# A decoder step on Trainium2: GpSimd makes every low part of the feed-forward weights, VectorE only the weight sums

## What is computed

```python
def conv_ffn(x, buf, w_up, conv_w, conv_b, w_down):
    u = x @ w_up                                   # 1024 -> 2 * 3072
    u_full = jnp.concatenate([buf.astype(u.dtype), u], axis=1)
    uc = causal_dwconv(u_full, conv_w, conv_b)     # width 3, per channel
    val, gate = uc[..., :D_FF], uc[..., D_FF:]
    return (jax.nn.gelu(gate) * val) @ w_down, new_buf
```

## Time and profile before

| what | before |
|---|---|
| median of 3 runs | 2521.88 us (2520.99 to 2522.19) |
| the profiled execution, its own time | 2521.42 us |
| its span, first to last instruction | 2519.5 us |
| TensorE busy | 2482.8 us, 99% of the span |
| VectorE busy | 1722.3 us, 68% |
| ScalarE busy | 1060.0 us, 42% |
| GpSimd busy | 852.7 us, 34% |
| chain that ended last | TensorE 79%, VectorE 5%, ScalarE 1% |
| mean granted TensorE clock | 0.998 of full speed |

### The profile page before, as it was taken

One profiled execution on the slowest core, in us unless ns is written; L12 is line 12 of the kernel. 1 busy time (PEld: TensorE's weight loads), 2 busy tenths in 40 slices (PEclk: granted clock), 3 DMA queues, 4 the chain that ended last, 5 costly groups with the idle time before them and its releaser, 6 DMA issues.

```text
span 2519.5 us, 41775 instructions
## 1 busy us (share of the span) xinstructions
PE 2482.8 (99%) x16340; PEld 2426.5 (96%) x16340; DVE 1722.3 (68%) x2796; ACT 1060.0 (42%) x1832; POOL 852.7 (34%) x527
## 2 busy tenths in 40 slices
PE   8999999999999999999999999999999999999998
PEld 7999999999999999998999999899999999999998
DVE  8877497666666666786655665649766666666678
ACT  5665253333333333334444444615333333333343
POOL 2001324344444333443333333032344443333341
PEclk9999999999999999999999999999999999999999
DMA  4111301111111111143233332411111111111112
GB/s 145 49 45 64 111 30 51 51 51 51 51 51 43 50 47 42 47 145 121 91 100 97 99 103 87 156 59 34 51 51 51 51 50 44 51 45 41 50 46 98
DMA packets 102769, 170.16 MB, mean 68 GB/s; under 512 B 11909, under 2 KB 50309, under 8 KB 102318
## 3 DMA queue, kind: packets, MB, share of 16 engines
q1 hardware_dynamic: 96622, 145.19, 18.1%
q10 hardware_dynamic: 5952, 22.30, 2.3%
HBM read 145.93 MB, written 26.23 MB: 68 GB/s over the span
## 4 chain that ended last, share of the span: by engine, by line
PE 79%; DVE 5%; ACT 1%; issue 1%; DVEq 0%; ACTq 0%
PE psum L1369 19%; PE psum L1225 13%; PE psum L1227 13%; PE psum L1226 13%; PE psum L1431 3%; PE psum L1435 3%; PE psum L1433 3%; PE psum L1465 2%; PE psum L1111 2%; PE psum L1489 2%; PE psum L1477 1%; PE psum L1668 1%; DVE line L2366 1%; DVE inverse_rms L2378 1%; DVE line L2326 0%
## 5 line engine op out<-in xcount | busy, mean ns | idle before, releaser
L742 POOL TENSOR_TENSOR w_lo<-w_raw,w_hi 128x512 fp32r<-128x512 f32 x232 | 372.9, 1608 | 771.6 <-ACT w_hi L1791 771.0
L1227 PE MATMUL psum<-xn_lo,w_hi 128*128 128x352 f32 x1568 | 506.7, 323 | 0.0
L1225 PE MATMUL psum<-xn_hi,w_hi 128*128 128x352 f32 x1568 | 506.3, 323 | 0.0
L1226 PE MATMUL psum<-xn_hi,w_lo 128*128 128x352 f32 x1568 | 505.6, 322 | 0.0
L1791 ACT ACTIVATE w_hi<-w_raw 128x512 fp32r<-128x512 f32 x294 | 184.5, 629 | 540.6 <-DVE w_raw L2612 313.4
L1369 PE MATMUL psum<-h_hi,w_hi 128*128 128x352 f32 x1032 | 332.8, 322 | 1.0 <-DVE x L2703 0.9
L1369 PE MATMUL psum<-h_hi,w_lo 128*128 128x352 f32 x1032 | 333.7, 323 | 0.0
L1369 PE MATMUL psum<-h_lo,w_hi 128*128 128x352 f32 x1032 | 332.9, 323 | 0.0
L1227 PEld LDWEIGHTS psum<-xn_lo,w_hi 128*128 128x128 f32 x1568 | 296.4, 189 | 0.0
L1225 PEld LDWEIGHTS psum<-xn_hi,w_hi 128*128 128x128 f32 x1568 | 295.1, 188 | 0.5 <-DVE line L2718 0.3
L1226 PEld LDWEIGHTS psum<-xn_hi,w_lo 128*128 128x128 f32 x1568 | 295.5, 188 | 0.0
(11 more groups left out here) (359 smaller groups left out, 5532.3 us busy)
## 6 DMA issues: line engine op xcount, KB each, us to landing
w_raw<-in_w SPq DMA_DIRECT2D x190, 256.0 KB, 2.7
w_raw<-in_w SPq DMA_DIRECT2D x56, 512.0 KB, 3.5
w_raw_third<-in_w SPq DMA_DIRECT2D x98, 256.0 KB, 2.9
k_pages<-in_cache_k SPq DMA_DIRECT2D x128, 64.0 KB, 2.0
v_pages<-in_cache_v SPq DMA_DIRECT2D x128, 64.0 KB, 2.0
scratch_line<-scratch_row ACTq DMA_DIRECT2D x1, 4608.0 KB, 21.3
x<-in_x SPq DMA_DIRECT2D x8, 528.0 KB, 8.4
scratch_x<-x ACTq DMA_DIRECT2D x1, 4224.0 KB, 13.5
```

What stands on the lines that cost most here:

```text
L742: return eng.tensor_tensor(out_lo, op_src(op), out_hi.bitcast(F32), ALU.subtract).then_inc(FS[l][LOW[op][0]], 1)
L1225: pe.matmul(out, op_hi(op)[:, k, :], hi, start=start, stop=False, skip_group_check=True)
L1226: pe.matmul(out, op_lo(op)[:, k, :], hi, start=False, stop=False, skip_group_check=True)
L1227: return pe.matmul(out, op_hi(op)[:, k, :], lo, start=False, stop=True, skip_group_check=True)
```

## The change

GpSimd makes the low parts of b11 and b21 of every pair as well, each in its place in the order of the operands. VectorE's `weight_low` is gone with its six calls. The separate semaphore `dve_lo` is gone: one semaphore, `op_lo`, counts all low parts in the order of the operands, and TensorE, VectorE and SyncE wait for an operand on that. `first_sums` and `fourth_sum` still wait for the low part of the operand that they write over, which now comes from GpSimd.

```diff
-def on_dve(op):
-    return op[0] in ("b11", "b21") and op[1] > 0
-
 def lows():
-    had, out = dict(op_lo=0, dve_lo=0), {}
+    had, out = dict(op_lo=0), {}
     for op in OP:
-        name = "dve_lo" if on_dve(op) else "op_lo"
+        name = "op_lo"
...
@@ GpSimd, ffn
-                    if not on_dve(op):
-                        low(l, op, op_hi(op), op_lo(op))
+                    low(l, op, op_hi(op), op_lo(op))
@@ VectorE
-            def weight_low(l, op):
-                dve.wait_ge(*FS[l].at("op_hi", OP[op] + 1))
-                low_part(dve, l, op, op_hi(op), op_lo(op))
...
-                weight_low(l, ("b11", 1))
                 if l == 0:
                     dve.wait_ge(rg_out, 32)
                 first_sums(l, 1)
-                weight_low(l, ("b21", 1))
                 inverse(r)
...
                     if ahead:
-                        weight_low(l, ("b11", f + 1))
                         first_sums(l, f + 1)
                     plain_third(f, 0)
                     if ahead:
-                        weight_low(l, ("b21", f + 1))
                         fourth_sum(l, f + 1)
...
                         conv_end(f, 0)
                         outs(0)
-                        weight_low(l, ("b11", f + 1))
...
                     if f < FT - 1:
                         first_sums(l, f + 1)
-                        weight_low(l, ("b21", f + 1))
                     outs(2)
```

More of the change, by code:

```diff
@@ L604, in program @@
         FULL = dict(u_state=2 * FT, u_used=2 * FT, tap_done=2 * FT, vc_ready=FT, gc_ready=FT, gg_ready=FT, hf_ready=FT,
-                    hh_ready=FT, hl_ready=FT, tail_out=16, op_hi=len(OP), op_lo=LOWS["op_lo"], dve_lo=LOWS["dve_lo"], mm=len(STEP),
+                    hh_ready=FT, hl_ready=FT, tail_out=16, op_hi=len(OP), op_lo=LOWS["op_lo"], mm=len(STEP),
                     w_sums=2 * (FT - 1), t3_sum=FT - 1, t4_sum=FT - 1, xh=KT, xl=KT, s_base=4, s_sum=16, s_hi=16, s_lo=16, copied=3 * (FT - 1),
```

## The result

| what | before | after |
|---|---|---|
| median of 9 runs each | 2522.12 us (2520.99 to 2523.47) | 2529.06 us (2528.09 to 2530.02) |
| the profiled execution, its own time | 2521.42 us | 2529.09 us |
| its span | 2519.5 us | 2527.3 us |

The changed kernel is slower by a quarter of a per cent, clear of the noise: ratio 1.0026, 95% interval 1.0018 to 1.0035, that is 6.9 us by the medians and 7.7 us between the two profiled executions. 6.8 us were forecast.

The account below looks back on a forecast made before the run. TensorE, busy 2482.8 of 2519.5 us, was taken as the bound, with VectorE the bound in the head of each block. Four places gave 3.4 us a layer, 6.8 in all, so 2528.7 us; range 2523 to 2533.

Parts of the forecast that it names:

- Head of a block: Pair 1: first sum waits for b11's low, b21's low delays the sums; reciprocal 1.1 us later a layer (bounds 0, 1.7).
- Pair 1 to pair 2: VectorE's chain 1.1 us late through to p6's copy; TensorE stands 0.86 us at p7 of pair 2 (bounds 0, 2).
- the slack of 0.24: Time between p6's copy ending and p7 of pair 2 starting, less 0.05 us for the semaphore: 0.24 us.
- Pair 22 to pair 23: Same order of work, some 1.0 us late against 0.54 of slack: 0.48 us a layer (bounds 0, 1.6).
- the sign that I named: Sign of a right forecast: TensorE gets a wait of 0.5 us at p7 of pair 23, in each layer.
- Down products of pair 2: Pair 3's two lows delay the first addition to x; the third output waits 0.95 us a layer (bounds 0, 1.6).
- Pairs 3 to 21 at 0: Steady pairs, 38 in all: second tap 0.92 us late, but third output still finds the addition done; cost 0.
- the bound of 0.24: Upper bound of the cost in pairs 3 to 21: 0.24 us a pair, 9 us in all.
- The sum: Four places of a layer: 1.1 + 0.86 + 0.95 + 0.48 = 3.4 us, 6.8 us in all.
- It disappears in the slack: Rival: collisions spared in two or three of four places; no measurable change, 0 to 5 us; chance 0.33.
- The steady pairs lose their cover: Rival: addition to x in pairs 3 to 21 over 1.14 us later; 2532.5 to 2537.8 us; chance 0.12.
- Faster: Rival: VectorE's relief of 63 us ends a wait; gain bounded to 0.2 us a layer in pair 1; chance 0.04.

Follow-up runs that it names:

- e1: Kernel before, with only the low parts of b11 and b21 of pair 1 (4 of the 92) on GpSimd; 2523.44 us, ratio 1.0005.
- e5: Changed kernel, but GpSimd makes b21's low part only when both first sums are done; 2524.91 us, ratio 1.0008 to the kernel before.
- e11: Changed kernel, with ScalarE's copies of p6 moved early in pairs 1, 2 and 23 as in e9; 2530.59 us, ratio 1.0031 to the kernel before.
- e2: Kernel before, with only the low parts of pairs 2 and 23 (8 of 92) on GpSimd; 2524.41 us, ratio 1.0008.
- e3: Kernel before, with only the low parts of pair 3 (4 of 92) on GpSimd; 2523.61 us, ratio 1.0005.
- e4: Kernel before, with only the low parts of pairs 4 to 22 (76 of 92) on GpSimd; 2524.01 us, ratio 1.0005.
- e8: e4 with b21's low part made twice, with the same values, in pairs 4 to 22; 2564.29 us (one run).
- e6: Kernel before, with only b21's low part of pair 1 (2 of 92) on GpSimd, behind the first sums; 2522.97 us, ratio 1.0001.
- e7: Kernel before, with ScalarE's copy of p6 in pair 1 right behind p5's, ahead of t3's high part; 2520.67 us, ratio 0.9992.
- e9: Kernel before, p6's copy before t3's high part in pair 1, right behind it in pairs 2 and 23; 2523.91 us, ratio 1.0003.
- e12: Kernel before, lows of pairs 3 to 22 (80 of 92) on GpSimd, b21's behind the two sums; 2523.98 us, ratio 1.0003.
- e10: e9 with e6's edit added (b21's low of pair 1 on GpSimd behind the sums); 2521.81 us, ratio 0.9996 to the kernel before.

## Why the prediction was right, step by step

- **Head of a block**: 1.1 forecast, 0.96 / 1.02 measured, and e1 alone gives 0.96 / 1.01. Idle 1.24 and a sum of 1.71, by the mechanism stated; e5 shows that b21's low is the part that costs, since without it the head is as before.
- **Pair 1 to pair 2**: 0.86 forecast, 0.53 / 0.65 measured. The mechanism and the place were right, the size was not. The step said that the full 1.1 us goes on from the second tap to p6's copy. Counted from p7 of pair 1 in layer 0, the second tap even starts 0.15 us earlier (13.12 against 13.27), since VectorE no longer makes two lows, one of them at 1.69, and its first tap is spared t2's low (1.32 against 1.94). That low meets the second tap now, which ends 0.76 later (15.36 against 14.60). Then b22's low, which met a small copy before (1.10 late), meets a tap (0.92), and the third sum is only 0.58 us later (19.80 against 19.22). With the slack of 0.24, which held, p7 is 0.34 us later (23.23 against 22.89). The copy as the bound was half the truth: e11 shows t3's low right behind it.
- **Pair 22 to pair 23**: 0.48 forecast, 0.32 / 0.33 measured, and 0.34 / 0.31 in e2. The same overestimate of what goes on; and the sign that I named, a wait of 0.5 us at p7 of pair 23, isn't among the listed waits: the 0.3 us lie in the starts of p7's first two matmuls (0.39 and 0.27 us behind the one before instead of 0.16).
- **Down products of pair 2**: 0.95 forecast, 1.07 / 1.01 measured; e3 alone gives 0.73 / 1.02. Right, with two collisions in front of the addition to x.
- **Pairs 3 to 21 at 0**: 0.34 / 0.38 measured, 0.02 us a pair, within the bound of 0.24. The second tap takes 2.25 us as forecast (before 1.33), the addition follows at once, and no wait of the third output is listed in these pairs. e4 repeats it, e8 shows where the cover ends.
- **Not in the sum**: 0.33 / 0.61 us behind pair 23. TensorE has new waits for additions to x there, 0.22 us in layer 0 and 0.68 in layer 1. The cause stays open: e1, e3, e6 and e7, which leave pairs 22 and 23 alone, repeat this stretch to 0.03 us, and runs that touch pair 23 scatter (e5 +0.31 / +0.18, e2 -0.72 / +0.34, e9, which moves no low part, +0.41 / +0.32).
- **The sum**: in a layer 0.4 to 0.5 us too much for pairs 2 and 23 together, 0.36 too little for the steady pairs, 0.3 to 0.6 for the tail. That the total of 6.8 came so near to 6.9 is luck in part: the terms' errors cancel, and one loss wasn't in the sum at all.

**The rivals.** *It disappears in the slack* fell: no collision was spared, waiting GpSimd went in ahead of VectorE's next instruction in every place that I read. No low took longer than 2.42 us, so none can have waited for two taps in a row (1.28 + 1.33 = 2.61). e5 is what it would have looked like. *The steady pairs lose their cover* fell: the tap is late by 0.92 (1.10 in two places), not by the low's 1.28, which is the rule of the Trainium skill named there, taken in full. The rows agree with that rule's direction (the first sum takes 0.69 alone in e5, and 1.71 beside a low in the changed kernel), not with its price at a tap. *Faster* fell: e12 takes nearly all of the relief without the collisions, and it is worth nothing; e6 shows the only gain on that side, 0.05 / 0.6 us at the reciprocal.

## What to carry to other kernels

A small elementwise operation moved from VectorE to GpSimd doesn't leave VectorE: where it met VectorE's taps, sums or small copies on SBUF, VectorE lost 0.6 to 1.1 us, mostly 0.9 and more, for 0.7 saved. Move it only beside PSUM evacuations (the one at 375.15 in the changed kernel takes 0.48 us beside t1's low, as the same one does alone), idle time or work that was seen to run beside it, as the reciprocal did here (one input alone is no safe sign: the copy of two columns has one too and lost 1.1), and say so with a wait on GpSimd rather than leave it to the order of the queue. Price such a change place by place, by the slack at the next wait of the bounding engine: 92 moved operations cost 7 us in five or six places of a layer, and 80 of them, placed well, cost nothing and gave nothing. And before a late result is moved up in a queue, look whether its source is ready there, and which second result of the same chain is late right behind it.

## What the runs showed that I had not expected

- A tap that meets a low loses 0.92 us in most places, a copy of two columns 1.1 (1.25 instead of 0.16) and a sum 1.0 (1.71 instead of 0.69): the price hardly depends on how long VectorE's own instruction is. It is less where the low has begun earlier: the fourth sum in pair 1 begins 0.44 us behind t1's low and takes 1.40, 0.71 more than alone.
- The reciprocal (6.75 us, one input) ran beside a low of 1.29 us in e5, e6 and e10, and neither was longer.
- The lower clock behind a wait of 2.7 us cost nothing in layer 1 and 3.4 us in layer 0 of one execution (e7), against 1.7 us before. That is 1.7 us of the time in either direction, as much as most of these edits, and it can pass for the effect of one (e2).
